# One of four convolution blocks of the first tile moved from VectorE to TensorE, and three projection groups placed beside the LayerNorm

## The reference, cut to what matters

```python
proj = x @ w_in                                    # q, k, v and u (2 x 512 columns)
attn = window_attention(rotary(q), rotary(k), v)   # chunks of 64, window 128, sinks
c_in = u[..., :512] * sigmoid(u[..., 512:])        # GLU
c_ext = concat([conv_prev, c_in], axis=1)          # conv_prev is zero for the prompt
c = depthwise_conv(c_ext, conv_dw_w, 31 taps) + conv_dw_b
c = silu(layer_norm(c, conv_ln_g, conv_ln_b))
mix = concat([attn, c], -1) @ w_out
h = layer_norm(ALPHA * x + mix, ln1_g, ln1_b)
up = h @ w_up                                      # 2 x 2816 columns
upc = depthwise_conv(concat([ffn_prev, up]), 3 taps)
f = (silu(upc[..., :2816]) * upc[..., 2816:]) @ w_down
ple = sigmoid(h @ w_pg + b_pg) * (p @ w_pe)
y = layer_norm(ALPHA * h + f + ple, ln2_g, ln2_b)
```

## Time and profile before

| | |
|---|---|
| median of 3 runs | 2485.96 us |
| profiled execution | 2489.22 us |
| its span, first to last instruction | 2487.4 us |
| TensorE busy | 2393.0 us, 96% |
| VectorE / ScalarE / GpSimd busy | 1449.9 / 1277.6 / 1606.6 us |
| chain that ended last | TensorE 85%, VectorE 6%, ScalarE 4% |
| mean granted TensorE clock | 0.982 |

### The profile page before, as it was taken

How to read it: one execution, slowest core, us unless ns; L and a number is a source line. 1 busy time by engine, 2 the same in 40 slices (tenths; PEclk the granted TensorE clock), 3 DMA queues, 4 the chain that set the end, 5 groups by cost and what they waited for, 6 DMA issues and landing times.

```text
span 2487.4 us, 38824 instructions
## 1 busy us (share of the span) xinstructions
PE 2393.0 (96%) x15109; PEld 2351.9 (95%) x15109; DVE 1449.9 (58%) x2338; ACT 1277.6 (51%) x2070; POOL 1606.6 (65%) x1284
## 2 busy tenths in 40 slices
PE   7789999999999999999999999999999999998996
PEld 7789998999999999999999999999899999988996
DVE  5747884467666357666626767652676665264432
ACT  4547555466444446644445654453565435355652
POOL 7447787775665676566567656656865655667773
PEclk9889999999999999999999999999999999999998
DMA  6324454543333444333344433334443332534442
GB/s 226 102 96 153 152 184 152 177 145 117 113 125 115 160 155 144 119 117 127 104 164 155 146 122 115 124 109 162 154 148 109 125 134 97 169 118 165 167 147 79
DMA packets 119046, 341.54 MB, mean 137 GB/s; under 512 B 15312, under 2 KB 43600, under 8 KB 118864
## 3 DMA queue, kind: packets, MB, share of 16 engines
q1 hardware_dynamic: 95408, 311.32, 37.2%
q10 hardware_dynamic: 23456, 27.74, 3.4%
HBM read 330.12 MB, written 8.99 MB: 136 GB/s over the span
## 4 chain that ended last, share of the span: by engine, by line
PE 85%; DVE 6%; ACT 4%; issue 2%; POOL 1%; DMA 1%; ACTq 0%; SPq 0%; DVEq 0%
PE ps L511 27%; PE ps L513 27%; PE ps L512 27%; DVE sq L1116 2%; POOL w_lo L462 1%; PE ps L602 1%; DMA w_raw<-in_panels 1%; ACT w_hi L630 1%; PE ps L550 1%; DVE acc L1053 1%; PE ps L581 1%; PE ps L569 1%; PE ps L559 1%; DVE res L1053 1%; DVE ps L1156 0%
## 5 line engine op out<-in xcount | busy, mean ns | idle before, releaser
L462 POOL TENSOR_TENSOR w_lo<-w_raw,w_hi 128x512 fp32r<-128x512 f32 (+1 forms) x1272 | 1605.6, 1289 | 842.3 <-ACT w_hi L630 840.8
L630 ACT CAST w_hi<-w_raw 128x1024 fp32r<-128x1024 f32 (+1 forms) x636 | 622.2, 981 | 605.9 <-PE ps L513 418.6
L511 PE MATMUL ps<-h_hi,w_hi 128*128 128x386 f32 (+5 forms) x2496 | 816.0, 327 | 9.6 <-DVE f_lo L994 4.1
L512 PE MATMUL ps<-h_lo,w_hi 128*128 128x386 f32 (+5 forms) x2496 | 807.6, 324 | 0.0
L513 PE MATMUL ps<-h_hi,w_lo 128*128 128x386 f32 (+5 forms) x2496 | 807.6, 324 | 0.0
L511 PEld LDWEIGHTS ps<-h_hi,w_hi 128*128 128x128 f32 x2496 | 473.6, 190 | 18.2 <-issue 9.4
L512 PEld LDWEIGHTS ps<-h_lo,w_hi 128*128 128x128 f32 x2496 | 474.3, 190 | 1.3
L513 PEld LDWEIGHTS ps<-h_hi,w_lo 128*128 128x128 f32 x2496 | 474.6, 190 | 0.0
L511 PE MATMUL ps<-f_hi,w_hi 128*128 128x384 f32 (+2 forms) x1264 | 412.0, 326 | 10.1 <-DVE f_lo L994 5.5
L512 PE MATMUL ps<-f_lo,w_hi 128*128 128x384 f32 (+2 forms) x1264 | 407.6, 322 | 0.0
L513 PE MATMUL ps<-f_hi,w_lo 128*128 128x384 f32 (+2 forms) x1264 | 407.5, 322 | 0.0
(11 more groups left out here) (128 smaller groups left out, 2025.2 us busy)
## 6 DMA issues: line engine op xcount, KB each, us to landing
w_raw<-in_panels SPq DMA_DIRECT2D x540, 512.0 KB, 3.2
w_raw<-in_panels SPq DMA_DIRECT2D x48, 384.0 KB, 3.0
w_raw<-in_panels SPq DMA_DIRECT2D x48, 128.0 KB, 2.3
xres<-in_xT ACTq DMA_DIRECT2D x32, 192.0 KB, 2.9
out_yT<-res ACTq DMA_DIRECT2D x4, 1536.0 KB, 6.5
a_raw<-in_xT ACTq DMA_DIRECT2D x6, 768.0 KB, 6.7
out_yT<-res ACTq DMA_DIRECT2D x2, 1024.0 KB, 4.9
x_raw<-in_xT SPq DMA_DIRECT2D x1, 1536.0 KB, 7.3
```

The lines of the kernel that those rows point to most:

```text
L462: ins = pool.tensor_tensor(w_lo[:, n % WS, c], w_raw[:, n % RS, c], w_hi[:, n % WS, c].bitcast(F32), ALU.subtract)
L511: pe.matmul(out, w_hi[:, sl, c], hi, start=k == 0, stop=False)
L512: pe.matmul(out, w_hi[:, sl, c], lo, start=False, stop=False)
L630: act.copy(w_hi[:, n % WS, 0:w], w_raw[:, n % RS, 0:w]).then_inc(w_hi_done, 1)
```

## The change

The fourth block (number 3, `HB - 1`) of the first tile's convolution is no longer made on VectorE. Instead ScalarE makes 31 diagonal matrices `diag[:, k, :]`, each the identity scaled by the weights of tap k, four after each of the groups 3 to 10 of the first tile (`diagonals`). TensorE multiplies each with the GLU output shifted by k and sums the 31 products in PSUM (`convolve`), in two pieces of 128 tokens. ScalarE adds the bias and copies the result out (`take_convolved`). `diag` lies in the memory of `h_hi` and `h_lo`, so the clearing of their first two columns moves behind the second piece.

Three `in` groups of the second tile (gate and value of block 3, and v) move from ahead of the LayerNorm to beside it: one behind `square`, two behind `lo`. The transposes of v, the scores, `turn` and `mixed` get other places among the six groups that are left. The remaining 93 taps get new counts.

```diff
-    left = [[0, 31], [1, 31], [2, 31], [3, 31]]
+    left = [[c, CONV_K] for c in range(HB - 1)]
...
         first_taps(head_taps.get(g, 0))
+        if 3 <= g < 11:
+            stage("diag", 4 * (g - 3))
...
-    ahead = {0: [("vt", 0)], 1: [("scores", 0, 0)], 4: [("turn", 0, 0)], 5: [("mixed", 0, 0)], 6: [("scores", 0, 1)]}
-    after = {2: [("divide", 0, 0)], 3: [("conv_add", 0, 0), ("conv_add", 0, 1)], 7: [("divide", 0, 1), ("conv_add", 0, 2)],
-             8: [("turn", 0, 1)]}
-    for n, g in enumerate(GLU + [IN_V]):
+    before = {0: [("conv_pe", 0)], 1: [("vt", 0), ("scores", 0, 0)], 3: [("turn", 0, 0), ("conv_pe", 1)],
+              4: [("mixed", 0, 0), ("scores", 0, 1)]}
+    behind = {0: [("conv_out", 0)], 2: [("divide", 0, 0)], 3: [("conv_out", 1), ("conv_add", 0, 0)], 4: [("conv_add", 0, 1)],
+              5: [("divide", 0, 1), ("turn", 0, 1)]}
+    for n, g in enumerate(GLU[:6]):
...
-        first_taps((9, 4, 8, 8, 10, 6, 10, 6, 4)[n])
+        first_taps((9, 6, 8, 8, 8, 1000)[n])
+    stage("conv_add", 0, 2)
     stage("mixed", 0, 1)
     stage("att_split", 0)
-    first_taps(1000)
-    stage("conv_add", 0, 3)
-    for name in ("tree", "mean", "centre", "square", "sqtree", "var", "root", "scale", "affine", "lo"):
+    for name in ("tree", "mean", "centre", "square"):
         stage(name, "cln", 0)
+    stage("in", 1, GLU[6])
+    for name in ("sqtree", "var", "root", "scale", "affine", "lo"):
+        stage(name, "cln", 0)
+    stage("in", 1, GLU[7])
+    stage("in", 1, IN_V)
...
                 else:
                     pe.wait_ge(att_done, unit_no(t, u))
+                    if t == 0:
+                        pe.wait_ge(conv_out, 2)
...
+            def convolve(piece):
+                if piece:
+                    pe.wait_ge(conv_out, 1)
+                    pe.wait_ge(probt_done, 1)
+                else:
+                    pe.wait_ge(diag_done, CONV_K)
+                    pe.wait_ge(glu_done, HB)
+                    pe.wait_ge(const_set, 1)
+                for k in range(CONV_K):
+                    c = piece * P + k
+                    mm = pe.matmul(ps[:, AUX + 1, 0:P], diag[:, k, :], g_in[:, HB - 1, c:c + P],
+                                   start=k == 0, stop=k == CONV_K - 1)
+                mm.then_inc(conv_pe, 1)
...
+            def diagonals(k0):
+                if k0 == 0:
+                    act.wait_ge(const_in, 16 * CONSTS)
+                for k in range(k0, min(k0 + 4, CONV_K)):
+                    act.activation(diag[:, k, :], ident[:], ACT.Copy, scale=prm("conv_w", (HB - 1) * CONV_K + k)
+                                   ).then_inc(diag_done, 1)
+            def take_convolved(piece):
+                act.wait_ge(conv_pe, piece + 1)
...
+                act.activation(a_raw[1][:, HB - 1, piece * P:piece * P + P], ps[:, AUX + 1, 0:P], ACT.Identity,
+                               bias=prm("conv_b", HB - 1)).then_inc(conv_out, 1)
+                if piece:
+                    act.copy(g_in[:, HB - 1, 0:HALO], g_in[:, HB - 1, LENS[0]:LENS[0] + HALO]).then_inc(halo_done, 1)
+                    act.wait_ge(zero_set, 1)
+                    act.copy(h_lo[:, :, 0:FHALO], h_keep[:])
+                    act.copy(h_hi[:, :, 0:FHALO], h_keep[:]).then_inc(h_halo, 1)
...
-            act.wait_ge(zero_set, 1)
-            act.copy(h_lo[:, :, 0:FHALO], h_keep[:])
-            act.copy(h_hi[:, :, 0:FHALO], h_keep[:]).then_inc(h_halo, 1)
```

More of the change, by code:

```diff
@@ L122, in plan @@
             stage("x_low", 1)
-    ahead = {0: [("vt", 0)], 1: [("scores", 0, 0)], 4: [("turn", 0, 0)], 5: [("mixed", 0, 0)], 6: [("scores", 0, 1)]}
-    after = {2: [("divide", 0, 0)], 3: [("conv_add", 0, 0), ("conv_add", 0, 1)], 7: [("divide", 0, 1), ("conv_add", 0, 2)],
-             8: [("turn", 0, 1)]}
-    for n, g in enumerate(GLU + [IN_V]):
-        for what in ahead.get(n, ()):
+    before = {0: [("conv_pe", 0)], 1: [("vt", 0), ("scores", 0, 0)], 3: [("turn", 0, 0), ("conv_pe", 1)],
[3 more added lines that the diff above has]
+    for n, g in enumerate(GLU[:6]):
+        for what in before.get(n, ()):
             stage(*what)
         stage("in", 1, g)
-        for what in after.get(n, ()):
+        for what in behind.get(n, ()):
             stage(*what)
-        first_taps((9, 4, 8, 8, 10, 6, 10, 6, 4)[n])
+        first_taps((9, 6, 8, 8, 8, 1000)[n])
+    stage("conv_add", 0, 2)
     stage("mixed", 0, 1)
     stage("att_split", 0)
-    first_taps(1000)
-    stage("conv_add", 0, 3)
-    for name in ("tree", "mean", "centre", "square", "sqtree", "var", "root", "scale", "affine", "lo"):
+    for name in ("tree", "mean", "centre", "square"):
         stage(name, "cln", 0)
+    stage("in", 1, GLU[6])
[3 more added lines that the diff above has]
+    stage("in", 1, IN_V)
     for i in range(NT):
@@ L607, in _ @@
                     group(e)
+                elif e[0] == "conv_pe":
+                    convolve(e[1])
                 elif e[0] == "vt":
@@ L704, in conv_input @@
                     act.copy(g_in[:, c, 0:HALO], g_in[:, c, LENS[t]:LENS[t] + HALO]).then_inc(halo_done, 1)
+            def diagonals(k0):
[6 more added lines that the diff above has]
+                act.wait_ge(conv_pe, piece + 1)
+                if piece == 0:
+                    act.wait_ge(const_in, 16 * CONSTS)
+                    computed(act, ("in", 0, N_IN - 1))
+                act.activation(a_raw[1][:, HB - 1, piece * P:piece * P + P], ps[:, AUX + 1, 0:P], ACT.Identity,
[5 more added lines that the diff above has]
+                    act.copy(h_hi[:, :, 0:FHALO], h_keep[:]).then_inc(h_halo, 1)
             def first_tap(e):
@@ L875, in _ @@
                         load_xres(e[1], e[2] + XS)
+                elif what == "diag":
+                    diagonals(e[1])
                 elif what == "x_load":
@@ L886, in _ @@
                     conv_input(*e[1:])
+                elif what == "conv_out":
+                    take_convolved(e[1])
                 elif what == "product":
@@ L1075, in convolved @@
                     ins = dve.tensor_tensor(a_raw[1][:, c, tok:tok + cnt], odd[:, col:col + cnt], even[:, col:col + cnt], ALU.add)
-                    if t == 0 and c == HB - 1:
+                    if t == 0 and c == HB - 2:
                         ins.then_inc(conv_done, 1)
```

17 lines of the change are left out of this document (12 added, 5 removed).

## The result

The changed kernel takes 2492.43 us, median of 8 runs (2490.15 to 2496.88), against 2485.94 for the kernel before in the same measurement. The ratio is 1.0033, 95% interval 1.0024 to 1.0042: **slower, by 6.5 us in the medians and by 8 by the ratio** (its interval is 6 to 10 us), where no change was forecast. The time lies above the forecast's own range of 2482 to 2490, just inside the wide one of 2479 to 2493, and at the place of the rival with the second piece at half clock. The profiled execution took 2491.96 us, its span is 2490.2, 2.8 longer than that of before; its clock is 0.986 against 0.982.

The account below looks back on a forecast made before the run. TensorE, busy 96% of the span, was taken to bound the kernel. Terms +0.7 + 14.9 + 5.7 - 4.2 - 0.3 + 0.9 - 15.9 - 1.8 summed to 0.0: forecast 2486.0 us, own range 2482 to 2490, wide range 2479 to 2493.

Parts of the forecast that it names:

- the rival with the second piece at half clock: Second convolution piece on TensorE takes 14.9 instead of 7.4 us, kernel slower at 2492.5 us; chance 0.11.
- The pieces: Convolution on TensorE: two pieces of 62 float32 records, 7.4 us each, adding 14.9 us that nothing hides.
- that rival: Weights do not load beside the convolution's matmuls: records 0.242 us apart, 15.1 us more, 2501 us; chance 0.08.
- The head: Before the first piece: ScalarE's diagonals delay a cast, GpSimd and TensorE's last head group; +0.7 us, between 0 and +2.5.
- The price of a batch: Four diagonal activations of 128x128 on ScalarE, forecast at 1.2 us, 0.30 each.
- The new waits: TensorE among the six groups: 2.7 before the scores, 1.7 before the second piece, 1.3 before the second scores; +5.7 us.
- The LayerNorm stretch: Sixth group's end to first `out` group takes 24.9 us; with three groups moved beside LayerNorm, 40.8 becomes 24.9: -15.9 us.
- the wait before the second `turn`: After the sixth group, VectorE does one GLU product and the divide before TensorE's second `turn`: 2.1 us.
- The clock: Among the six groups: half clock after the scores' wait, -0.3 us against before; a coin's chance before the second piece, +0.9.
- the faster rival: Clock stays up through waits, first sum at full clock, shorter records, diagonals hidden: -6.4 us, 2479.6 us; chance 0.27.
- The start of the `out` groups: First `out` groups after LayerNorm start at full instead of half clock, after a short wait: -1.8 us.
- -4.2: TensorE's old wait before the scores, 4.16 us for the mask VectorE writes behind the copy of v, goes away.

Follow-up runs that it names:

- diag_early: Changed kernel with 24 of the 31 diagonals made in ScalarE's earlier idle time, seven behind groups 3 and 4; ratio 1.0023 to the kernel before, 2490.89 us.
- one_diagonal_batch: Changed kernel with only the first four diagonals made and reused for all taps, so another convolution; ratio 1.0021 to the kernel before, 2491.01 us.
- divide_ahead: Changed kernel with the two softmax divides placed one stage earlier on VectorE; ratio 1.0016 to the kernel before, 2490.08 us.
- groups_not_moved: Changed kernel with the three second-tile groups ahead of the LayerNorm again, convolution of block 3 still on TensorE; ratio 1.0061 to the kernel before, 2502.07 us.
- changed_again: The changed kernel, unchanged, measured and profiled once more; ratio 1.0036 to the kernel before, 2496.14 us.
- the control: The kernel before, unchanged, measured against itself and profiled again; ratio 1.0002, 2485.82 us.

## Why the prediction was wrong

**The pieces: right.** 14.9 forecast; 7.08 and 7.16 in the trace. The weights load beside the matmuls: 62 records in 7.08 are 0.114 each, half of the 0.226 of the earlier trace rows, so that rival is refuted.

**The head: mis-sized.** +0.7 forecast, +3.1 measured (first piece at 60.33; the transposes of v stood just ahead of 57.58). The cast of panel 13 came at 49.78, 2.6 later than before, which is about what I had said. But VectorE splits the second tile's input from 49.91 to 53.27 (3.36 us, both inputs in SBUF), and GpSimd's panel, started at 50.90, ended 2.5 us behind that: 4.91 instead of my 3.5. Before, one of the panel's halves was nearly done when the split began. Then TensorE had waited 3.09 us, and most of the group ran at half clock, 4.5 instead of 3.0 us. diag_early and one_diagonal_batch show the cause of the wait: with ScalarE free, it is 1 us again. The half clock is luck in part: in divide_ahead the group ran at full clock behind a wait of 3.10. The price of a batch was right (1.28 for 1.2), though the overlap that I read for its low end was not: two copies in 0.98 against 0.58 for one overlap by 0.18, not 0.09.

**The new waits: right in the ones I named** (2.58, 1.25, 1.24 for 2.7, 1.7, 1.3). One was missing: 1.39 before the first `turn`, whose divide stands behind taps that wait for ScalarE's copy, and two groups cover it where three did.

**The LayerNorm stretch: the step that failed.** -15.9 forecast. The stretch took 28.6 us in the first profile (-12.2) and 30.0 in the second (-10.8), instead of 24.9. The term in it is the wait before the second `turn`: 2.1 forecast, 3.99 measured, since the divide takes 3.4 us beside GpSimd's panels. Where GpSimd was not at work when it began, in one_diagonal_batch and groups_not_moved, it took 1.65 and the wait was 2.22: what the forecast lacked in this term is the collision. I had priced it by the earlier trace rows, the 1.86 of a wait elsewhere, where the divide had begun before TensorE was done. What ran beside it I did not ask. After that wait `turn` and `mixed` ran at half clock, 1.0 and 0.9 more, where I had counted half clock for the first sum alone; in changed_again it reached into the moved group as well. divide_ahead took this away, and the stretch was 23.1.

**The clock: a coin in more places than one.** I gave the fall behind the second piece's wait one half, +0.9. It fell in all but one of the profiles that have this wait (8.79, or 10.11 behind a longer one). At the scores, where I had counted on it for 2.0 us, it did not fall in most profiles: they took 1.59, and in all of these but the first the fall came later, in the groups behind. The rival "second piece at half clock" named the place and the time that was measured, but not the mechanism: granted 0.94 over the 28 us around it, in changed_again the clock was at half for some 3.3 us, and the piece lost 1.6, not 7.4. That the median fell on its number is luck. For the faster rival I had said that GpSimd suffers less beside fewer taps; it did not suffer from them: in the first profile a half panel beside the eleven taps of 63.02 took 1.28 us (63.74), and one with no VectorE instruction beside it 1.29 (131.25).

**The start of the `out` groups: right.** -1.8 forecast; from the first `out` group to the next sum it was 24.8 before, 23.1 now.

**The sum.** In the first profile +3.1, +14.2, +6.5, -4.2, the fallen clock of before gained back (-2.3), -12.2 and -1.7 give +3.4; the next sum starts at 163.89 against 160.38, +3.5. In changed_again it starts at 168.59 against 159.53 in the control, +9.1. The median difference, 6.5, lies between. Of the 5.6 us between 9.1 and 3.5, 0.9 is the difference between the two profiles of before, and 4.7 that between the two of the changed kernel. Nor does what stands there stand at the end to the last, as I had it: the two profiles of before part by 3.0 us more behind it. One profile of each kernel would have told +2.8.

## What to carry to other kernels

When work moves to the engine that bounds, count the waits that its dependences put in the new order, and give the next few microseconds at half clock a price: here the matmuls cost 11 us, what they were to save came back only in part, and where the same instructions stand was worth 17 us. A slow instruction may also hide in a collision of two engines that a shift of 1.5 us in a third one makes or undoes. An instruction's price depends on what its neighbour does at that moment: look for a GpSimd instruction beside every VectorE instruction with two SBUF inputs on the chain. And where a clock falls in some executions only, one profile is one sample.

## What the runs showed of the hardware

The same VectorE addition of 128x8 took 1.14 us beside GpSimd's subtraction and 0.16 without it, the product of 128x1024 2.01 and 1.23; the other way round GpSimd's panel of two halves took 4.91 beside a VectorE subtraction of 3.36 us. In one_diagonal_batch and groups_not_moved, with the same order on VectorE and GpSimd idle at that moment, the addition took 0.16 or 0.15. The Trainium skill's page SBUF — State Buffer (section Who interferes with whom) says that a VectorE instruction with two SBUF inputs contends with a GpSimd instruction that reads SBUF, and that the contention is an exclusive lock; the trace agrees in size: from 50.90 to the end of the split at 53.27, then 2.5 for two halves.

TensorE's granted clock fell to half in one execution and not in the other behind a wait of 1.25 us that followed eight transposes and a wait of 1.39 or 1.18. With a group between the transposes and the piece it did not fall, in the one profile taken of that.

Four activations of 128x128 with a scale per partition took 1.28 us, and 24 in a row 7.13 in diag_early, so 0.3 each.
